# Attention values as one stationary block of high and low halves, and the neighbourhood bias added on TensorE

## The reference, cut to what matters

```python
# A: multi-head attention, 8 heads of 96 (query, key) and 64 (value)
s = jnp.einsum('bqhd,bkhd->bhqk', q, k).astype(jnp.float32) * scale
p = jax.nn.softmax(s, axis=-1).astype(v.dtype)
return jnp.einsum('bhqk,bkhd->bqhd', p, v)
# B: neighbourhood attention, 4 heads of 64, an 8x16 window on the 64-wide grid, plus all context keys
s_loc = (s_loc + bias.astype(jnp.float32)).reshape(B, H, GRID_W, kr * kc)
p = jax.nn.softmax(jnp.concatenate([s_loc, s_ctx], axis=-1), axis=-1).astype(v.dtype)
```

## Time and profile before

| | us |
|---|---|
| median of 3 runs | 3155.1 (3154.56 to 3157.39) |
| profiled execution, its time | 3152.75 |
| profiled execution, its span | 3151.2 |
| PE (TensorE matmul) busy in the span | 3005.9 (95%) |
| DVE (VectorE) busy | 1641.4 (52%) |
| ACT (ScalarE) busy | 917.2 (29%) |
| POOL (GpSimd) busy | 223.2 (7%) |

### The profile page before, as it was taken

How to read it: one execution, slowest core, us unless ns; L and a number is a source line. 1 busy time by engine, 2 the same in 40 slices (tenths; PEclk the granted TensorE clock), 3 DMA queues, 4 the chain that set the end, 5 groups by cost and what they waited for, 6 DMA issues and landing times. The chain is left out here.

```text
span 3151.2 us, 44954 instructions
## 1 busy us (share of the span) xinstructions
PE 3005.9 (95%) x17054; PEld 2608.0 (83%) x17054; DVE 1641.4 (52%) x2910; ACT 917.2 (29%) x1433; POOL 223.2 (7%) x252
## 2 busy tenths in 40 slices
PE   7999999989988899999999899999998989999999
PEld 3888888878978787888888788888876979778887
DVE  4664466444466736652664566255244467643333
ACT  2221122123366522211222222112222367432221
POOL 1300000021213100000000000000002123000000
PEclk9999999999999999999999999999999999999999
DMA  7543243212100023332432234233212200223332
GB/s 240 124 126 100 80 126 106 81 53 56 44 13 1 26 61 104 112 112 65 127 116 85 67 113 134 59 111 100 72 50 67 66 12 7 67 80 106 88 96 91
DMA packets 412202, 263.55 MB, mean 84 GB/s; under 512 B 11700, under 2 KB 403672, under 8 KB 412088
## 3 DMA queue, kind: packets, MB, share of 16 engines
q1 hardware_dynamic: 407256, 253.14, 26.9%
q0 software_dynamic: 2752, 4.66, 0.9%
q10 hardware_dynamic: 2080, 4.19, 0.4%
HBM read 256.13 MB, written 6.68 MB: 83 GB/s over the span
## 5 line engine op out<-in xcount | busy, mean ns | idle before, releaser
L406 PE MATMUL pair<-h_hi,w_hi 128*128 128x512 f32 x2912 | 1029.9, 354 | 46.9 <-DVE h_lo L529 23.2
L407 PE MATMUL pair<-h_lo,w_hi 128*128 128x512 f32 x2912 | 963.4, 349 | 0.0
L410 PE MATMUL pair<-h_hi,w_lo 128*128 128x512 f32 x2912 | 819.9, 350 | 0.0
L406 PEld LDWEIGHTS pair<-h_hi,w_hi 128*128 128x128 f32 x2912 | 555.3, 191 | 181.6 <-issue 46.5
L407 PEld LDWEIGHTS pair<-h_lo,w_hi 128*128 128x128 f32 x2912 | 555.5, 191 | 73.3
L380 DVE TENSOR_TENSOR w_lo<-w_raw,w_hi 128x1024 fp32r<-128x1024 f32 (+1 forms) x276 | 362.7, 1315 | 307.5 <-ACT w_hi L373 301.0
L410 PEld LDWEIGHTS pair<-h_hi,w_lo 128*128 128x128 f32 x2912 | 471.8, 192 | 19.8
L373 ACT ACTIVATE w_hi<-w_raw 128x1024 fp32r<-128x1024 f32 (+1 forms) x276 | 307.8, 1116 | 614.1 <-PE pair L410 589.0
L406 PE MATMUL pair<-s_hi,w_hi 128*128 128x512 f32 x1232 | 426.6, 346 | 0.0
L407 PE MATMUL pair<-s_lo,w_hi 128*128 128x512 f32 x1232 | 400.5, 344 | 0.0
L647 DVE SCALAR_TENSOR_TENSOR mod_acc<-mod_raw,cs,mod_acc 128x256 f32<-128x256 f32 x896 | 365.3, 480 | 0.0
(11 more groups left out here) (215 smaller groups left out, 3390.7 us busy)
## 6 DMA issues: line engine op xcount, KB each, us to landing
mod_raw<-in_w_mod SPq DMA_DIRECT2D x64, 1024.0 KB, 5.0
w_raw<-in_w_ffn_gate SPq DMA_DIRECT2D x88, 512.0 KB, 3.8
w_raw<-in_w_ffn_up SPq DMA_DIRECT2D x88, 512.0 KB, 3.8
w_raw<-in_w_ffn_down SPq DMA_DIRECT2D x64, 704.0 KB, 4.6
w_raw<-in_w_in SPq DMA_DIRECT2D x32, 512.0 KB, 4.0
w_raw<-in_w_out SPq DMA_DIRECT2D x12, 512.0 KB, 4.1
w_raw<-in_w_q_up SPq DMA_DIRECT2D x8, 576.0 KB, 4.1
mod_first<-in_w_mod ACTq DMA_DIRECT2D x2, 2048.0 KB, 12.3
```

The costliest lines, as they stand in the source:

```text
L406: eng.matmul(dst, wh, rh, start=first, stop=False)
L407: eng.matmul(dst, wh, rl, start=False, stop=False)
L410: last = eng.matmul(dst, wl, rh, start=False, stop=end)
```

## The change

Values. v_hi and v_lo become one tensor `v_both` in which each head's 64 hi columns and 64 lo columns stand side by side (for na heads `vn_both`, one tensor per pair of heads). A key chunk of PV is now two matmuls in place of three: one with the whole 128-column block against pt_hi, which puts hi·hi in psum2 partitions 0 to 63 and lo·hi in 64 to 127, and one with the 64 hi columns against pt_lo, into partitions 0 to 63. The two partition halves of psum2 are added at the end: ScalarE copies one half to y_f, VectorE adds the other, waits for that, and multiplies.

Bias. For each na head the table is split in na_hi and na_lo (ScalarE copies, VectorE subtracts; na_lo is written over na_tt), and TensorE adds both to the scores by two 512-column matmuls with an identity as stationary operand. VectorE's addition and copy into prob go away, and the maximum and the exponential read the scores in PSUM. The splits of the tables stand at steps 2 and 4, and at two steps in the na part. A second identity `ident_r` is made at the start.

```diff
-        v_hi = sb("v_hi", [P, TOK // P, MLA_HEADS * V_DIM], F32R, "sarea", 0)
-        v_lo = sb("v_lo", [P, TOK // P, MLA_HEADS * V_DIM], F32R, "sarea", 4 * TOK * 4)
+        v_both = sb("v_both", [P, TOK // P, MLA_HEADS, 2 * V_DIM], F32R, "sarea", 0)
...
+        def bias_at(l, s):
+            nb = att_chunks(l)
+            per = nb // 2
+            return {2: (0, 0), 4: (0, 1), 4 * nb + per + 2: (1, 0), 5 * nb + 2: (1, 1)}.get(s)
...
@@ attention_pe
+                    if biased(l, s):
+                        eng.wait_ge(bias_lo_done, bias_tables(l, s))
                     for a, b in keys:
                         dst, q = pair[s % 2][:, a:b], slice(q0, q0 + P)
                         eng.matmul(dst, qh[rows, q], kh[rows, a:b], start=True, stop=False)
                         eng.matmul(dst, qh[rows, q], kl[rows, a:b], start=False, stop=False)
+                        if biased(l, s) and a == 0:
+                            first = (BIAS_SLOTS // 2 - 1 - 2 * (q0 // P)) * GRID_W
+                            for table in (na_hi, na_lo):
+                                eng.matmul(dst, ident_r[:, :], table[:, j, first:first + SEQ], start=False, stop=False)
                         last = eng.matmul(dst, ql[rows, q], kh[rows, a:b], start=False, stop=True)
...
-                        eng.matmul(dst, vh[:, k, i * P:(i + 1) * P], ph, start=k == kc[0], stop=False)
-                        eng.matmul(dst, vh[:, k, i * P:(i + 1) * P], pl, start=False, stop=False)
-                        last = eng.matmul(dst, vl[:, k, i * P:(i + 1) * P], ph, start=False, stop=k == kc[-1])
+                        first, end = k == kc[0], k == kc[-1]
+                        if first:
+                            eng.matmul(dst, vals[:, k, :], ph, start=True, stop=False)
+                        last = eng.matmul(dst[0:V_DIM], vals[:, k, 0:V_DIM], pl, start=False, stop=False)
+                        if not first:
+                            last = eng.matmul(dst, vals[:, k, :], ph, start=False, stop=end)
@@ attention_act
-                    eng.activation(y_f[r, i if kind == "mla" else 4 + i, q0:q0 + 2 * P], psum2[r, bank:bank + 2 * P],
+                    eng.activation(y_f[r, i if kind == "mla" else 4 + i, q0:q0 + 2 * P], psum2[other, bank:bank + 2 * P],
                                    ACT.Copy).then_inc(a_copied, 1)
...
+                if bias_at(l, s):
+                    i, j = bias_at(l, s)
+                    eng.wait_ge(tt_loaded[j], 16 * (2 * l + i + 1))
+                    eng.activation(na_hi[:, j, :], na_tt[:, j, :], ACT.Copy).then_inc(bias_hi_done, 1)
@@ attention_dve
-                    if not own_scores(l, s):
...
-                        eng.tensor_tensor(prob[:, s % 3, 0:SEQ], pair[s % 2][:, 0:SEQ], na_tt[:, j, first:first + SEQ],
-                                          ALU.add).then_inc(a_bias, 1)
-                        eng.tensor_copy(prob[:, s % 3, SEQ:TOK], pair[s % 2][:, SEQ:TOK]).then_inc(a_bias, 1)
-                        eng.wait_ge(a_bias, bias_steps(l, s) + 2)
...
+                if bias_at(l, s):
+                    i, j = bias_at(l, s)
+                    eng.wait_ge(bias_hi_done, 4 * l + 2 * i + j + 1)
+                    eng.tensor_tensor(na_lo[:, j, :], na_tt[:, j, :], na_hi[:, j, :].bitcast(F32), ALU.subtract)\
+                       .then_inc(bias_lo_done, 1)
...
                     eng.wait_ge(a_copied, c0 // 2 + b + 1)
+                    eng.tensor_tensor(y, y, psum2[r, bank:bank + 2 * P], ALU.add).then_inc(a_added, 1)
+                    eng.wait_ge(a_added, c0 // 2 + b + 1)
                     eng.tensor_tensor(y, y, psum2[r, bank + 2 * P:bank + 4 * P], ALU.mult).then_inc(a_out, 1)
```

More of the change, by code:

```diff
@@ L263, in program @@
         vn_f = sb("vn_f", [P, TOK // P, NA_WIDTH], F32, "sarea", na_at + 4 * TOK * 4)
-        v_hi = sb("v_hi", [P, TOK // P, MLA_HEADS * V_DIM], F32R, "sarea", 0)
-        v_lo = sb("v_lo", [P, TOK // P, MLA_HEADS * V_DIM], F32R, "sarea", 4 * TOK * 4)
+        v_both = sb("v_both", [P, TOK // P, MLA_HEADS, 2 * V_DIM], F32R, "sarea", 0)
         y_f = sb("y_f", [P, 6, TOK], F32, "harea", KD * TOK * 4)
-        vn_hi = sb("vn_hi", [P, TOK // P, NA_WIDTH], F32R, "sarea", 14 * TOK * 4)
-        vn_lo = sb("vn_lo", [P, TOK // P, NA_WIDTH], F32R, "sarea", na_at + 4 * TOK * 4)
+        vn_both = [sb(f"vn_both{i}", [P, TOK // P, 2, 2 * NA_DIM], F32R, at, off * TOK * 4)
+                   for i, (at, off) in enumerate((("harea", 4), ("sarea", 14)))]
         wo_first = sb("wo_first", [P, 2, KD * P], F32, "sarea", 8 * TOK * 4)
@@ L350, in program @@
         a_hi, a_lo, v_hi_done = sem("a_hi"), sem("a_lo"), sem("v_hi_done")
-        a_s, a_max, a_exp, a_rsum, a_copied, a_t, a_pth, a_ptl, a_pv, a_out, a_bias = (
-            sem(f"a_{k}") for k in ("s", "max", "exp", "rsum", "copied", "t", "pth", "ptl", "pv", "out", "bias"))
+        a_s, a_max, a_exp, a_rsum, a_copied, a_t, a_pth, a_ptl, a_pv, a_out = (
+            sem(f"a_{k}") for k in ("s", "max", "exp", "rsum", "copied", "t", "pth", "ptl", "pv", "out"))
+        a_added = sem("a_added")
+        bias_hi_done, bias_lo_done, ident_ready = sem("bias_hi_done"), sem("bias_lo_done"), sem("ident_ready")
         a_latent_t, a_latent_hi, a_latent_lo = (sem(f"a_latent_{k}") for k in ("t", "hi", "lo"))
@@ L1115, in unit_values, with token_values @@
             return pair[o.odd][:, :].rearrange("p (h d) -> p h d", d=NOPE + V_DIM)[:, :, NOPE:]
-        def token_values(v, t):
-            return v[:, t, :].rearrange("p (h d) -> p h d", d=V_DIM)
+        def token_values(half, t):
+            return v_both[:, t, :, half * V_DIM:(half + 1) * V_DIM]
         def pool_parts(l):
@@ L1517, in splits, with biased, bias_tables @@
             i = g - MLA_HEADS
[L1518 to L1523, removed]
-            kind, _, _, q0, _ = chunk_info(l, c)
-            return kind == "mla" or q0 >= SEQ
+            values = vn_f[:, :, i * P:(i + 1) * P].rearrange("p k (j d) -> p k j d", j=2)
+            return 2 * MLA_HEADS + 3 * i, [(na_f[:, i, 0:w], qh[:, 0:w], ql[:, 0:w]), (na_f[:, i + 2, :], kh[:, :], kl[:, :]),
+                                           (values, vn_both[i][:, :, :, 0:NA_DIM], vn_both[i][:, :, :, NA_DIM:])]
+        def biased(l, c):
+            kind, _, _, q0, _ = chunk_info(l, c)
+            return kind == "na" and q0 < SEQ
+        def bias_tables(l, c):
+            kind, i, j, _, _ = chunk_info(l, c)
+            return 4 * l + 2 * i + j + 1
+        def bias_at(l, s):
+            nb = att_chunks(l)
+            per = nb // 2
+            return {2: (0, 0), 4: (0, 1), 4 * nb + per + 2: (1, 0), 5 * nb + 2: (1, 1)}.get(s)
         def latent_parts(l, c):
@@ L1531, in latent_parts @@
                        if chunk_info(layer, x)[3] < SEQ)
-        def bias_steps(l, c):
-            return sum(2 for layer in range(l + 1) for x in range(c if layer == l else n_chunks(layer))
-                       if not own_scores(layer, x))
         Y_ORDER = [0, 1, 2, 3, 6, 7, 4, 5]
@@ L1646, in attention_act @@
                             eng.wait_ge(a_t, c0 + c + 1)
-                        eng.activation(pt_hi[:, a // P:b // P, c % 4, :], pmid[:, a:b].rearrange("p (k q) -> p k q", q=P),
+                        eng.activation(pt_hi[:, a // P:b // P, c % 4, :],
+                                       pmid[:, a:b].rearrange("p (k q) -> p k q", q=P),
                                        ACT.Copy).then_inc(a_latent_hi if a == 0 else a_pth, 1)
@@ L1733, in attention_dve @@
                             eng.wait_ge(a_pth, c0 + c + 1)
-                        eng.tensor_tensor(pt_lo[:, a // P:b // P, c % 4, :], pmid[:, a:b].rearrange("p (k q) -> p k q", q=P),
+                        eng.tensor_tensor(pt_lo[:, a // P:b // P, c % 4, :],
+                                          pmid[:, a:b].rearrange("p (k q) -> p k q", q=P),
                                           pt_hi[:, a // P:b // P, c % 4, :].bitcast(F32), ALU.subtract)\
@@ L1871, in _ @@
                 first_mod_load(act, n)
+            act.wait_ge(const_loaded, 16)
+            act.activation(ident_r[:, :], ident[:, :], ACT.Copy).then_inc(ident_ready, 1)
             act.wait_ge(acc_free[0], 1)
```

32 lines of the change are left out of this document (14 added, 18 removed).

## The result

| | before | after |
|---|---|---|
| median of 4 runs, us | 3154.83 | 3202.86 |
| lowest to highest, us | 3150.8 to 3157.39 | 3199.82 to 3204.21 |
| span of the profiled execution, us | 3151.2 | 3202.6 |

The changed kernel is 48 us slower, ratio 1.0152 with a 95% interval from 1.0134 to 1.017. That is about half of the 97 us of the forecast's sum, and 6 us above the time that the first rival (columns change at no cost) gave. The profiled spans differ by 51.4 us, and the two attention stages, summed from the first group of transposes (T) to the last, by 54.1 (351.7 before, 405.8 after): the loss lies there, and the rest of the span is 2.7 us shorter.

A forecast was written before the change was run, and what follows sets the result against it. The larger of chain and TensorE bound most attention steps, VectorE some in layer 0's neighbourhood part. Terms 17.6 + 20.1 + 20.4 + 18.2 + 20 + 1 = 97 gave 3252 us (66%, own range 3225 to 3290); 8 in 10: 3185 to 3290.

The forecast's parts named there:

- the first rival: In PV, the stationary operand changes between 128 and 64 columns at no cost: sum +42, 3197 us; chance 17%.
- splits: Eight table splits in the attention stages make VectorE wait for ScalarE and delay T: +20 us together, +23 with columns free.
- chain: T, pt_hi, pt_lo, next T, with an output between in even steps; the addition to y_f lengthens it 0.46, 3.30 to 3.76.
- changes in partitions: Score and bias matmuls switch between 64 and 128 partitions: 0.165 us each, 64 added; a biased chunk's scores cost 0.80 more.
- I take 0.165, because it is the same array being cut in another direction: In PV, each change between 128 and 64 columns costs 0.165 us; about 520 changes, 86 us.
- +0.66 and +0.99 a half-pair: Column changes in PV: four in a pair's first half cost 0.66 us, six in its second 0.99.
- 3.76 and 3.45: Multi-head part of layer 1: forecast even step 3.76 us, set by the chain, and odd step 3.45, set by TensorE.
- multi-head part, both layers: Multi-head part with columns free: +1.8 us in layer 1 and +1.8 in layer 0.
- bias matmuls, neighbourhood: Neighbourhood part with columns free: 0.80 - 0.35 a step, +7.2 us in layer 1 and +7.2 in layer 0.
- 5.1 to 5.6: Neighbourhood splits at steps 2 and 4, without an output: steps of 5.1 to 5.6 us against 2.9 to 3.5.
- a rival of its own: TensorE's clock falls to a mean of 0.8 over the attention, losing 50 us more: 3300 us; chance 7%.
- the 0.9 that the prediction named: Sign in the attention stages: PEclk, TensorE's granted clock, would not be under 0.9.

## Why the prediction was right and wrong

**The sign and the place** were right: slower, all of it in the attention stages, with splits, chain and changes in partitions as causes.

**The step that failed** is "I take 0.165, because it is the same array being cut in another direction". It costs nothing: the starts are 0.12 apart in the changed kernel, and the time is the same without those changes. With it fall +0.66 and +0.99 a half-pair. It was the term with no row of its own, bounded at zero and at 0.165, and I took the end nearest to a row and to a rule; that end carried 86 us of TensorE's work into a sum of 97. The same sum with columns free is the first rival's, 42; the measured loss is 48. Because steps are the larger of chain and TensorE, less than that came out of it: multi-head, layer 1, was 3.62 to 3.75 and 2.44 a step, not 3.76 and 3.45.

**The rival's terms against what was measured** (regions from T to T; the parts are divided at the T in whose step the first neighbourhood scores stand):

| term | rival | measured |
|---|---|---|
| multi-head part, both layers | 3.6 | 4.7 |
| bias matmuls, neighbourhood | 14.4 | 12.7 |
| splits | 23 | 36.6 |

The first two rows are the regions of the kernel with GpSimd's splits less those of before; the last is the changed kernel less the one with GpSimd's splits. The sum is that of the regions, 54.1. That the rival's 3197 came within 6 us of the median is in part luck: the regions are 12 us over its sum, mostly for the lower clock that it left out, while the rest of the span is 2.7 us shorter and the profiled spans differ by 3.4 more than the medians.

**The chain** was right in mechanism and size: 0.45 us for the addition (0.46 forecast), of which 0.32 to 0.45 reach an even step, and in even steps T does wait for pt_lo. What the forecast didn't see is how much stood behind it: it treated the chain as a cost of the change, while the output's place ahead of pt_lo cost the kernel before 15 us already and the changed one 36.5.

**Changes in partitions**: 0.165 forecast, 0.19 to 0.21 measured; steps of 4.08 and 3.60 are what 3.58 - 0.35 + 0.80 = 4.03 and 3.11 - 0.35 + 0.80 = 3.56 give without the price of columns.

**The splits**: the stall itself was right, 6.87 for 6.9 in the neighbourhood part, 5.61 and 5.39 for "5.1 to 5.6" at the first head of layer 1. Over all eight, the stalled steps are 22.3 us longer than the same steps with GpSimd's splits, for 20 in the sum. Mis-sized was the term as a whole, 20 against 36.6, because the sum left out the steps behind, at a lower clock, and kept that for a rival of its own at the price of a mean of 0.8 over both stages. The mean stayed at 0.93 and 0.90 over 888 to 1106 and 2553 to 2770 (0.96 in both before), though over 2670 to 2770 it was 0.85, under the 0.9 that the prediction named. In the neighbourhood part of layer 1 the changed kernel takes 16.4 us more than with GpSimd's splits. Its two stalls account for 2.5 and 2.8 (6.59 and 6.87, both against 4.08). The four steps at the lower clock are 26.8 us instead of 15.4, and the two behind them 0.9 more; 1.3 goes off again, because with GpSimd the steps behind the two splits are 4.2 instead of 3.6.

**What stays open.** What brings the lower clock is not known. Moving the splits took both the stalls and the long stretch behind the last one away, but a stall by itself does not fix what follows: in the changed kernel one of 2.44 us of idle was followed by the full clock and one of 2.72 by 30.6 us at the lower. The kernel with one shape in the value matmuls, whose splits are the same, has the same two stalls (6.60 and 6.87); the two steps behind the first were 6.39 and 5.14, and behind the second 5.09 and then 4.06, no longer slow. Its median is within 1 us of the changed kernel's all the same. The mean clock of a whole execution is known for every run: 0.969 to 0.972 in the changed kernel, 0.969 to 0.973 in the one just named, and 0.977 to 0.980 with GpSimd's splits (0.975 to 0.978 in the kernel before). So every run of the changed kernel had more of the lower clock; where it fell is known of the profiled one alone. The stretch of 30.6 us cost some 12 us in that run; that the others paid it at the same place is not shown.

## What to carry to other kernels

Before a saving on one engine is added up, ask of each step whether that engine ends it; here 36.8 us of TensorE's work were gone and the kernel was 7 us slower, until two small operations moved behind the one that T waits for. That move was worth 15 us to the kernel before as well, and even behind it the blocks brought 12.8. A cost that no row shows should not carry a sum just because its nearest row looks alike: give both ends a like chance, or name the one row that would settle it. And a one-off of 1 us placed ahead of a chain costs its wait too, and in some runs a slower TensorE behind it: put it on an engine that has time to spare, even at twice the duration.

## What the runs showed of the hardware that was not expected

- TensorE alternates stationary operands of 128x64 and 128x128 without a gap (0.12 us from start to start at 256 columns), while 64x128 beside 128x128 costs 0.165 (before) to 0.21 us a change.
- After a gap of 2.72 us TensorE, busy almost without a break (30.32 of 30.6 us), stayed at the lower clock (0.51) for all of that time; after a gap of 2.44 us, 18 us earlier in the same run, it kept the full clock.
- A subtraction of 896 columns took 1.09 us on VectorE and 2.1 on GpSimd.
